# A hybrid decoder layer on one core: the second piece's dense work ends 14 slots earlier

## The reference, cut to what matters

```
proj = rmsnorm(x) @ w_in                      # conv, RG-LRU, SSD, gates follow from it
x = x + (sigmoid(g_a)*y_a + sigmoid(g_b)*y_b) @ w_out
tb = rmsnorm(x);  q = tb @ w_q;  s = einsum(q, sub_keys)         # scores
sv, si = top_k(s, 16);  fv, fi = top_k(sv[..0..] + sv[..1..], 16)    # "route": 8 heads x 16 rows a token
act = gelu(einsum('thkd,td->thk', u_emb[idx], tb))
x = x + einsum('thk,thkd->td', softmax(fv)*act, v_emb[idx])
```

## Time and profile before

| | |
|---|---|
| median of 3 runs | 2313.4 us |
| lowest, highest | 2299.11, 2315.27 us |
| the profiled execution's own time | 2313.13 us |
| its span, first to last instruction | 2311.3 us |
| mean granted clock of TensorE | 0.835 |
| busy: PE, DVE, ACT, POOL | 1692.4, 1536.0, 592.8, 920.7 us |
| bytes moved | 798.81 MB, mean 346 GB/s |

### The profile page before, as it was taken

One profiled execution on the slowest core, in us unless ns is written; L12 is line 12 of the kernel. 1 busy time (PEld: TensorE's weight loads), 2 busy tenths in 40 slices (PEclk: granted clock), 3 DMA queues, 4 the chain that ended last, 5 costly groups with the idle time before them and its releaser, 6 DMA issues.

```text
span 2311.3 us, 30904 instructions
## 1 busy us (share of the span) xinstructions
PE 1692.4 (73%) x10511; PEld 1161.4 (50%) x10511; DVE 1536.0 (66%) x4028; ACT 592.8 (26%) x1778; POOL 920.7 (40%) x840
## 2 busy tenths in 40 slices
PE   7899977687899899887899889996534344343434
PEld 7799976543588677665677667673100000000000
DVE  4534178777568546888656776545479778877865
ACT  5546255300144223445222341111011000010001
POOL 0000001155434554544454455566544444445442
PEclk9999999767899999999999999998666656655566
DMA  7487767299999999887899999998999999999996
GB/s 255 128 277 257 247 200 267 87 317 399 400 398 387 398 409 387 321 348 232 293 399 351 349 391 375 403 402 332 387 422 421 422 421 421 421 420 405 413 413 250
DMA packets 181934, 798.81 MB, mean 346 GB/s; under 512 B 20977, under 2 KB 21233, under 8 KB 147857
## 3 DMA queue, kind: packets, MB, share of 16 engines
q0 software_dynamic: 119808, 570.48, 62.8%
q1 hardware_dynamic: 59616, 219.40, 26.0%
q10 hardware_dynamic: 2352, 6.95, 1.0%
HBM read 779.88 MB, written 12.14 MB: 343 GB/s over the span
## 4 chain that ended last, share of the span: by engine, by line
PE 21%; DMA 15%; DVE 12%; issue 5%; POOL 2%; ACT 1%; POOLq 0%; DVEq 0%; another core or an unknown queue 0%; SPq 0%; ACTq 0%
PE ps L492 9%; DMA s_exr<-in_uv,s_gidx 6%; PE ps L819 3%; PE ps L802 3%; DVE s_exr L1741 3%; DMA s_wr<-in_uv,s_gidx 2%; DMA s_exr<-in_v,s_gidxT 2%; PE ps L475 2%; DMA s_hnr<-in_uv,s_gidx 1%; DMA s_xr<-in_uv,s_gidx 1%; POOL s_exr L1404 1%; DMA s_scr<-in_uv,s_gidx 1%; DVE s_wr L1741 1%; PE ps L845 1%; PE ps L614 1%
## 5 line engine op out<-in xcount | busy, mean ns | idle before, releaser
L492 PE MATMUL ps<-s_hnr,s_wr 128*128 128x256 f32 (+2 forms) x3968 | 669.0, 326 | 43.4 <-ACT s_hist_p L984 24.4
L492 PEld LDWEIGHTS ps<-s_hnr,s_wr 128*128 128x128 f32 x3968 | 599.2, 194 | 123.5 <-issue 73.6
L1359 POOL DMA_INDIRECT s_exr<-in_u,s_gidx x288 | 307.4, 1067 | 830.3 <-DVE s_act_z L1741 446.7
L1741 DVE CUSTOM_DVE_ANT_0 s_exr<-s_exr,s_tbg 128x1024 f32<-128x1024 f32 x407 | 491.3, 1221 | 192.3 <-DMA s_exr<-in_u,s_gidx 130.9
L1371 POOL DMA_INDIRECT s_exr<-in_v,s_gidxT x256 | 276.3, 1079 | 172.0 <-issue 86.9
L819 PE MATMUL ps<-s_exr,s_sw 128*32 128x512 f32 x476 | 156.7, 1040 | 168.7 <-DVE s_sw L1770 168.7
L1404 POOL DMA_INDIRECT s_exr<-in_uv,s_gidx x119 | 141.1, 1185 | 152.7 <-PE ps L819 122.5
L1179 ACT ACTIVATE s_gth<-s_g 128x4 f32<-128x4 f32 x64 | 13.1, 205 | 617.0 <-DVE s_g L1759 617.0
L802 PE MATMUL ps<-s_exr,s_zb 128*32 128x512 f32 x1072 | 146.0, 656 | 29.5 <-DMA s_exr<-in_v,s_gidxT 26.2
L1452 DVE SCALAR_TENSOR_TENSOR s_scr<-s_scr,s_par 128x128 f32<-128x128 f32 (+2 forms) x288 | 122.1, 426 | 47.6 <-ACT s_scr L990 39.0
L819 PEld LDWEIGHTS ps<-s_exr,s_sw 128*32 128x32 f32 x476 | 25.1, 157 | 249.7 <-DVE s_sw L1770 196.9
(11 more groups left out here) (319 smaller groups left out, 2722.2 us busy)
## 6 DMA issues: line engine op xcount, KB each, us to landing
s_wr<-in_wstream SPq DMA_DIRECT2D x360, 512.0 KB
s_tbg<-s_h2e ACTq DMA_DIRECT2D x36, 128.0 KB
s_exr<-in_u,s_gidx POOLq DMA_INDIRECT x288
s_exr<-in_v,s_gidxT POOLq DMA_INDIRECT x268
s_xr<-in_sample_h_in SPq DMA_DIRECT2D x8, 512.0 KB, 7.3
s_scr<-in_sample_h_in SPq DMA_DIRECT2D x8, 512.0 KB
out_sample_h_out<-s_xr SPq DMA_DIRECT2D x8, 512.0 KB
out_sample_h_out<-s_scr SPq DMA_DIRECT2D x8, 512.0 KB
```

The lines of the kernel that those rows point to most:

```text
L492: last = pe.matmul(ps[:, o % 2, 0:n], wring[:, slot, k, :], rhs[:, k, :], start=k == 0, stop=k == KT - 1)
L1359: pool.indirect_dma_start(uring[n % URING], None, a["u"], bass.IndirectOffsetOnAxis(ap=gidx[:, i % 2, s:s + 1], axis=0)).then_inc(u_in[n % ...
L1741: dve.tensor_tensor_reduce(out=u, in0=u, in1=tbg[:, i % 2, :], scale=1.0, scalar=0.0, op0=ALU.mult, op1=ALU.add, accum_out=act_z[:, i % 2, ...
```

## The change

Piece 1's dense work ends at slot 12 of group 3 in place of slot 26, and group 4's route is moved from slots 21 to 31 of group 3 to slots 13 to 31. Piece 2 starts where piece 1 ends and still ends at slot 26 of group 8, where the edge is as it was. `due_slots()` then spreads piece 1 over slots 0 to 108 and piece 2 over 108 to 282.

```diff
-EDGE_SLOT, EDGE_END = 21, 26
+EDGE_SLOT = 21
+PIECE_END = (0, 12, 26)
 ROUTE = ((2, 4, 6, 8, 10), (13, 15, 17, 19, 21))
-EDGE_ROUTE = ((EDGE_SLOT, 22, 23, 25, 26), (27, 28, 29, 30, 31))
+EDGE_ROUTE = {EDGE[0]: ((13, 15, 17, 19, 21), (23, 25, 27, 29, 31)),
+              EDGE[1]: ((EDGE_SLOT, 22, 23, 25, 26), (27, 28, 29, 30, 31))}
...
-        end = SLOTS * EDGE[pc.p - 1] + EDGE_END if pc.p else 0
+        end = SLOTS * EDGE[pc.p - 1] + PIECE_END[pc.p] if pc.p else 0
...
-                        if s == (EDGE_ROUTE if i in EDGE else ROUTE)[j][3]:
+                        if s == EDGE_ROUTE.get(i, ROUTE)[j][3]:
                             softmax_exp(2 * (i + 1) + j)
...
-                    for j, at in enumerate(EDGE_ROUTE if i in EDGE else ROUTE):
+                    for j, at in enumerate(EDGE_ROUTE.get(i, ROUTE)):
                         if s == at[0]:
                             route_keys(i + 1, j, 0)
```

## The result

The changed kernel takes 2317.8 us (median; 2310.5 to 2324.3 over 21 runs). Against the kernel before (21 runs beside it, of which one of 6653.8 us is left out) it is 1.0025 times as long, with an interval of 1.0013 to 1.0036, so 3.0 to 8.3 us slower, 5.8 in the middle. The forecast was 2303 us, 10 us faster. The range of 2284 to 2328 holds the result, and "within 1%" was the likeliest class, but the sign is wrong.

A forecast was written before the change was run, and what follows sets the result against it. Gathers and weights bound B, VectorE and its TensorE hand-overs C, the dense-step chain A; in D TensorE and DMA were near their limits. A -4, B -26, C +7, D +13 gave -10 us: 2303 us, range 2284 to 2328.

The forecast's parts named there:

- D: Slots 171 to 282, piece 2 after `xbc` and `ssd`: ten more slots cost +13 us, bounds +5 and +28.
- rival 1: D is full: transfers can't pass 378 GB/s, ten slots cost 28 us; +5 us, 2318 us; chance 0.2.
- A: Slots 0 to 28, `xbc`, `ssd`, `samp` of piece 1: three slots fewer give -4 us, bounds 0 and 8 gained.
- B: Slots 28 to 122, rest of piece 1, bound by gathers and weights: 11 slots fewer give -26 us, bounds 14 and 38.
- net nothing: Half a route, about 10 us of VectorE, lands in D, where VectorE's free time was to hide it.
- the bytes fit: `sr` in D: four more slots make 60.0 MB, 150 us at 400 GB/s; priced at +6 us with some waiting.
- C: Slots 122 to 171, `xbc` and `ssd` of piece 2, bound by VectorE: four more slots cost +7 us, bounds 5 and 14.
- The second edge: After 1581.1 us, with the wide groups: keeps its order and work, costed at nothing.
- the looser spacing: Group 4's route spread over more slots: 0 to 5 us, left in the range.
- Rival 2: No stretch is full; engines set the pace everywhere, 1.3 us a slot: +2 us, 2315 us; chance 0.15.
- Rival 3: D and C are free, +5 us each, A -5, B -35: -30 us, 2283 us; chance 0.15.
- rival 4: The weave doesn't move because dense steps lag behind their due slots: 2313 us; chance 0.05 with the unforeseen.

The follow-up runs named there:

- the last pair: Kernel before and changed kernel, both with four slots after each `sr` step and half of each weight unit loaded from `gb` of piece 2: D 19.6 us longer.
- in fours: Exactly four slots after each `sr` step of piece 2: kernel before 2331.8 us (0.9998), in more rounds 2330.9 us (0.998); changed kernel 2336.3 us (1.0002).

## Why the prediction was wrong, by its own steps

**The marks set out beforehand.** Slot 108 came at 876.2 us (878 foreseen), slot 161 at 1107.9 (1108), slot 282 at 1589.2 (1571). D's rate stayed at 378 GB/s, which was the mark of rival 1; it was to rise to 390. So the places are right up to D, in part by luck: slot 0 came 5.9 us late, and A and B together gave 7.8 us more than forecast.

**The step that failed is the price of D's ten slots.** I bounded it by 5 and 28 us, took +13 "nearer to the TensorE end, since TensorE holds most of the chain", and it measured +31.7 (+35.4 in the mean of four traces), over the upper bound. Two things were wrong in it.

*The choice between the ends.* That TensorE held most of the chain in a stage at 392 GB/s didn't mean that the next bytes were hidden. The step worked with 403 GB/s as the most, and made of that a cost of 2 us for two slots. With two slots `gb`/`z` took 4.9 (8.9 in the mean of eight traces), with ten 25.8: the rate stopped at 397 and 402, and a good part of the chain moved to the rows (16% on v rows with two slots more, 36% on u and v rows with ten; none before). TensorE and the DMA engines were both at their end, so the price was at least the dearer one, 2.6 to 4.4 us a slot, and not one between.

*What a slot carries.* The upper bound took the bytes alone, as if all other work went on beside them. VectorE's busy time shows what else moved: in D 277.0 to 298.4 us, +21.5 for ten slots, which is 2.15 a slot and not the 1.3 of the dot product. The rest is the half route that the prediction had seen to land in D and called "net nothing". In B the busy time fell by 24.2 us for eleven slots: 14 for the slots, and 10 for the half that left. So the gain of that half lay in B, where VectorE was not the bound, and its cost in D, where `sr` alternates between VectorE's scans, TensorE's steps and the rows. What the half alone costs there was not measured. That `sr` was priced at +6 because "the bytes fit" is the worst single term: it took +19.4 at 350 GB/s, 50 under the rate that I had let it reach. As I read it, means over the stage hid that the three take turns.

Shown: that the ten slots cost 31 to 39 us in D in every order tried, that part of it goes with the bytes and some 2.0 us a slot without them, that neither the `s_zb` wait nor the rhythm of `sr` carries it. Only argued: that the 2.0 us are VectorE's added work. TensorE's granted clock in D fell from 0.98 to 0.95 too, and its 14.8 us of added busy time in the last pair are a rival that no run separates from VectorE's 22.8.

**B, -26 of -31.5.** Right in mechanism. The rate stayed at 392 GB/s as "near 395" said, 2.9 us a slot, 2.5 us beyond my "at an unchanged rate" of 29. The waits for u rows in B fell from 64.0 us to 54.5, which is small beside the 24 us that my bound of 38 took. The part that I held back for TensorE in `seq` and `z` was not lost. In the three slower sessions B gave less: six traces with the early end have 398.9 to 411.2 us (mean 405.0), six without it 426.2 to 428.9 (427.4), so 22.4 us or 2.0 a slot.

**A, -4 of -6.3, and C, +7 of +8.3.** Right within 2.3 us. The +7 for C was right by its added margin for hand-overs; the price of 1.3 us a slot was not found: with four slots it is 2.1, with 14 it is 2.8.

**The second edge.** It was costed at nothing and gave 5.2 us; it is 57.6 to 61.7 us in all kernels with the early end and 61.7 to 64.7 in all those without. It has the same work. Why it is shorter stays open, and it isn't why the sign is wrong.

**The route.** "0 to 5 us for the looser spacing" was 0 as far as the runs tell.

**The rivals.** Rival 1 gave 2318 us, the measured time, but by -26 and +28 where -31.5 and +31.7 were found, and half of its mechanism: with bytes to spare D was still dear. Its own deciding point stands, though: D had to stay under 472.6 us and took 481.3. Rival 2's +2, 2315 us, was nearly as near in time, and B's 31.5 us with its rate kept rules its mechanism out. Rival 3 fell with D, and rival 4 with the places of the slots, which moved as planned. The argument against rival 1, that B moves 408 and 410 GB/s, spoke of stages in which TensorE had gaps (busy 65.2 of 72.6 and 60.7 of 65.6 us); in `gb`/`z` of D it had none.

**The rule weighed in the prediction.** No stage with dense work beside it went over 410 GB/s in the two main traces, and the wide groups reach 422 on the page after:

```profile
GB/s 252 130 274 256 240 181 272 82 309 409 393 387 363 404 409 356 379 263 220 384 395 357 365 345 381 410 389 359 417 422 422 421 421 421 420 412 411 405 422 244
```

By the 435 GB/s of the Trainium skill (page "DMA: Bandwidth & Descriptors", section "Where 436 GB/s comes from") `gb`/`z` with two more slots would have had room: 46.5 MB in 113.3 us are 410 GB/s, an estimate. It took 118.2 to 124.7 us at 397 GB/s and less, and with ten more slots it stood at 402. The room that counted ended below the highest rate seen in stages of the same kind, 410, which was in the earlier trace rows.

## What to carry to other kernels

Moving a unit of work from one stretch to another pays only by the difference of two prices, and each price is what all that travels with the unit (here its gathers, its quad and half a route) does to the engines that take turns in that stretch; here they were 2.9 us given and 3.2 us taken. A stage in which two resources both stand over 0.95 is to be priced with at least the dearer of the two prices from the first added unit on, whichever holds the chain today; here that was so. And a long wait that a trace shows is tested by removing it and reading the sum of the stretch: a wait of 15 us and 24 us of a stage were removed here, and within a session the ratio moved by 0.23% at most, inside its interval. Look also whether the wait was there before the change, and whether the edit removed it or only moved it.

## What the runs showed of the hardware that was not expected

**TensorE after a wait of 15 us.** Stretches of the changed kernel around the wait for `s_zb` (1372.9 to 1387.5 us): before, across and behind it.

```profile
1355.00:1374.00 19.00, 15.58 (x79) 11.85 (x77) 11.86 (x27) 7.05 (x14) 12.87 (x11) 1.00 0.88 329
1374.00:1391.00 17.00, 3.51 (x16) 0.59 (x16) 10.99 (x36) 5.08 (x9) 8.53 (x8) 0.50 1.03 377
1391.00:1408.00 17.00, 17.00 (x86) 12.57 (x82) 11.14 (x32) 2.45 (x5) 10.31 (x10) 1.00 0.95 358
```

The granted clock stood at its lower level, 1.2 GHz (0.50), through the wait, and the quad behind it took 3.64 us where the one ahead took 1.92. In the stretch behind it stood at 2.4 GHz again. D's mean of 0.95 against 0.98 comes from such places: in D the clock's record has 17 us at the lower level before and 44 us after, of which this place is 17.

**One chip, two sessions.** The kernel before took 2311.4 us in one session and 2332.3 in another on the same chip, 0.9% apart. In the traces the difference shows above all in `wq` of piece 2, 75.0 to 80.7 us in the one kind of session and 81.8 to 93.0 in the other; where it comes from no run here tells.

**Half-sized loads.** Leaving out half of D's weight bytes took 45 to 55 GB/s off its rate (368 or 378 to 323) and only 10 us off its 462; in fours it took 2 to 7 us off (450.8 and 456.1 to 448.7).
